# Down-projection in a fused two-block kernel: block sums by adding transfers, pairs of block buffers, one more turn by seven products

## The reference

```python
h2 = rmsnorm_2(x, norm2_g[l])
u = causal_dwconv(jnp.einsum('bsd,df->bsf', h2, w_up[l]), conv_w[l], conv_b[l])
u_gate, u_val = u[..., :D_FF], u[..., D_FF:]
x = x + jnp.einsum('bsf,fd->bsd', jax.nn.silu(u_gate) * u_val, w_down[l])
```

## Time and profile before

| | |
|---|---|
| median of 3 runs | 2071.07 us (2070.58 to 2071.88) |
| profiled execution | 2070.34 us, its span 2068.3 us |
| PE busy | 2062.9 us, 9896 matmuls |
| DVE busy | 1657.0 us |
| ACT busy | 1172.5 us |
| POOL busy | 51.8 us |
| HBM read | 420.57 MB, 204 GB/s over the span |

### The profile page before, as it was taken

How to read it: one execution, slowest core, us unless ns; L and a number is a source line. 1 busy time by engine, 2 the same in 40 slices (tenths; PEclk the granted TensorE clock), 3 DMA queues, 4 the chain that set the end, 5 groups by cost and what they waited for, 6 DMA issues and landing times.

```text
span 2068.3 us, 25511 instructions
## 1 busy us (share of the span) xinstructions
PE 2062.9 (100%) x9896; PEld 1732.2 (84%) x9896; DVE 1657.0 (80%) x1864; ACT 1172.5 (57%) x1398; POOL 51.8 (3%) x55
## 2 busy tenths in 40 slices
PE   9999999999999999999999999999999999999999
PEld 7888888888888887888888888888888888888887
DVE  7888788887887876887788778867777777789986
ACT  6766555555556555656555555555555555555553
POOL 0000000000000000110000000000000000000000
PEclk9999999999999999999999999999999999999999
DMA  9667777787674667655565656455555565556663
GB/s 348 206 199 225 222 233 226 210 244 221 247 263 153 218 207 213 207 179 182 154 231 180 210 182 218 160 184 181 188 190 191 190 195 183 192 184 233 226 202 131
DMA packets 118007, 424.33 MB, mean 205 GB/s; under 512 B 13184, under 2 KB 13952, under 8 KB 117632
## 3 DMA queue, kind: packets, MB, share of 16 engines
q1 hardware_dynamic: 109440, 394.66, 56.5%
q0 software_dynamic: 5472, 19.93, 5.6%
q10 hardware_dynamic: 2976, 8.14, 1.1%
HBM read 420.57 MB, written 2.10 MB: 204 GB/s over the span
## 4 chain that ended last, share of the span: by engine, by line
PE 99%; DMA 0%; ACT 0%; DVE 0%; ACTq 0%; issue 0%; DVEq 0%
PE g L938 51%; PE xs L984 10%; PE xs L791 8%; PE g L791 8%; PE g L988 7%; PE g L762 4%; PE xs L797 4%; PE g L797 4%; PE xs L840 1%; PE xs L1025 1%; PE xs L1161 0%; PE g L963 0%; PE xs L1158 0%; DMA par<-in_params 0%; PE xs L1178 0%; PE xs L1102 0%
## 5 line engine op out<-in xcount | busy, mean ns | idle before, releaser
L1859 DVE TENSOR_TENSOR w_lo<-raw,w_hi 128x1024 fp32r<-128x1024 f32 x625 | 757.3, 1221 | 290.9 <-ACT w_hi L1364 283.2
L1364 ACT ACTIVATE w_hi<-raw 128x1024 fp32r<-128x1024 f32 x625 | 655.7, 1057 | 508.4 <-PE g L938 221.6
L938 PE MATMUL g<-w_hi,in_both 128*128 128x512 f32 x1104 | 350.5, 390 | 0.0
L938 PE MATMUL g<-w_hi,mid_both 128*128 128x512 f32 x928 | 300.2, 393 | 0.0
L938 PEld LDWEIGHTS g<-w_hi,in_both 128*128 128x128 f32 x1104 | 207.3, 188 | 42.9
L938 PE MATMUL g<-w_lo,in_both 128*128 128x512 f32 x552 | 214.8, 389 | 0.0
L938 PEld LDWEIGHTS g<-w_hi,mid_both 128*128 128x128 f32 x928 | 174.2, 188 | 36.2
L938 PE MATMUL g<-w_lo,mid_both 128*128 128x512 f32 x464 | 180.6, 389 | 0.0
L791 PE MATMUL g<-mlp_both,w_hi 128*128 128x512 f32 x704 | 167.0, 391 | 0.0
L791 PE MATMUL xs<-mlp_both,w_hi 128*128 128x512 f32 x704 | 165.6, 390 | 0.0
L791 PEld LDWEIGHTS xs<-mlp_both,w_hi 128*128 128x128 f32 x704 | 130.7, 188 | 26.2
(11 more groups left out here) (532 smaller groups left out, 3439.5 us busy)
## 6 DMA issues: line engine op xcount, KB each, us to landing
raw<-in_stream SPq DMA_DIRECT2D x625, 512.0 KB, 4.3
d_block<-in_stream SPq DMA_DIRECT2D x28, 512.0 KB, 4.5
o_block<-in_stream SPq DMA_DIRECT2D x24, 512.0 KB, 4.7
v_block<-in_stream SPq DMA_DIRECT2D x20, 512.0 KB, 4.7
gm_block<-in_stream SPq DMA_DIRECT2D x16, 512.0 KB, 5.6
ge_block<-in_stream POOLq DMA_DIRECT2D x15, 512.0 KB, 5.5
ge_block<-in_stream SPq DMA_DIRECT2D x10, 512.0 KB, 4.6
gl_block<-in_stream POOLq DMA_DIRECT2D x6, 512.0 KB, 5.4
```

The source lines that it names most:

```text
L938: ins = mm(GG[:, bank, :], a[:, kt, t * P:(t + 1) * P], w[:, slot, half_chunk(j)], start=n == 0 and opens(item, bank), stop=ended and n == ...
L1364: activation(w_hi[:, n % RING, :], of[:], ACT.Copy).then_inc(hi_ready, 1)
L1859: v.tensor_tensor(w_lo[:, n % RING, :], of, w_hi[:, n % RING, :].bitcast(F32), ALU.subtract).then_inc(lo_ready, 1)
```

## The change

The down phase gets the other form. In each turn by products two block sums are now transfers that add, and the other two stay on DVE. There are two pairs of block buffers, used in turn, and the loads for a turn by products are issued one such turn earlier (two ahead in place of one). The four chunks of a mixed step now all stand between product 5 and product 7, in the order `MIXED_SPREAD`. In column group 1 a fifth turn goes by products: turn 10 with the chunks of turn 8, while turn 7's chunks go with the products of turn 6. With it comes one more set of sums of f. Column group 0 keeps its three mixed steps.

```diff
     "down": (((3, None), (4, None), (8, None), (9, None), (5, 0), (6, 1), (7, 2), (10, None)),
-             ((3, 0), (7, None), (4, 1), (5, 2), (8, 6), (9, None), (10, None))),
+             ((3, 0), (4, 1), (5, 2), (7, 6), (8, 10), (9, None))),
...
-SUMS_AT = {"v": (4, 8), "out1": (2, 6), "vv": (-7,), "down": (3, 7, 11, 64), "gm0": (-8, -5), "out2": (-7,)}
+SUMS_AT = {"v": (4, 8), "out1": (2, 6), "vv": (-7,), "down": (3, 7, 11, 64, 76), "gm0": (-8, -5), "out2": (-7,)}
...
-SPREAD = ("ug", "vv", "side")
+SPREAD = ("ug", "vv", "side", "down")
+TWO_SUMS = ("vv", "side", "down")
...
 MIXED = (1, "C0", 5, 7, "C1", 6, 3, "C2", 4, 2, "C3")
...
+MIXED_SPREAD = (1, 5, "C0", "C1", "C2", 3, "C3", 7, 6, 2, 4)
...
+def second_pair(q):
+
+    return QUADS[q][0] == "down" and (q - quads_ahead("down")) % 2 == 1
...
 def buffer_of(q, b):
 
+    if QUADS[q][0] == "down":
+        return b + 2 * second_pair(q)
...
-                if next_in_place(item) is not None and quad_of(item) + 1 < len(QUADS):
-                    q = quad_of(item)
-                    if QUADS[q + 1][0] == item.phase:
+                after = 2 if item.phase == "down" else 1
+                if next_in_place(item) is not None and quad_of(item) + after < len(QUADS):
+                    q = quad_of(item) + after
+                    if QUADS[q][0] == item.phase:
                         sp.wait_ge(lo_ready, n + 1)
-                        load_block(q + 1, next_in_place(item))
+                        load_block(q, next_in_place(item))
...
-                elif item.phase in MID_ORDER and item.product == 2:
+                elif item.phase in TWO_SUMS and item.product == 2:
                     dve.wait_ge(lo_ready, n + 1)
-                    to = wide(item.phase, item.group).blocks[B11]
+                    to = wide(item.phase, item.group).blocks[buffer_of(quad_of(item), B11)]
                     v.tensor_tensor(to[:], to[:], raw[:, CHUNK_COUNT[n] % RING, :], ALU.add).then_inc(sem["block_sums"], 1)
```

More of the change, by code:

```diff
@@ L282, in loads_of_block @@
 def loads_of_block(q, b):
-    return sum(phase not in SPREAD or b in (B11, B12) for phase, _, _ in QUADS[:q + 1])
+    return sum(not second_pair(k) and (QUADS[k][0] not in SPREAD or b in (B11, B12)) for k in range(q + 1))
+def second_pair(q):
+    return QUADS[q][0] == "down" and (q - quads_ahead("down")) % 2 == 1
 def spread_quads(q):
@@ L310, in sums_made @@
 def sums_made(q, p):
-    ahead = sum(1 if phase == "ug" else 2 if phase in MID_ORDER else 4 for phase, _, _ in QUADS[:q])
-    return ahead + ({5: 1, 4: 2} if QUADS[q][0] in MID_ORDER else {5: 1, 7: 2, 6: 3, 4: 4})[p]
+    ahead = sum(1 if phase == "ug" else 2 if phase in TWO_SUMS else 4 for phase, _, _ in QUADS[:q])
+    return ahead + ({5: 1, 4: 2} if QUADS[q][0] in TWO_SUMS else {5: 1, 7: 2, 6: 3, 4: 4})[p]
 def buffer_of(q, b):
+    if QUADS[q][0] == "down":
+        return b + 2 * second_pair(q)
     return b if b == B21 or QUADS[q][0] in SPREAD else (b + q - quads_ahead(QUADS[q][0])) % 3
@@ L652, in build, with block_in @@
     block_full = [sem[f"block_full{b}"] for b in range(4)]
+    second_full = [sem[f"second_full{b}"] for b in (B11, B12)]
+    def block_in(q, b):
+        if second_pair(q):
+            return second_full[b], 16 * ((q - quads_ahead("down")) // 2 + 1)
+        return block_full[b], 16 * loads_of_block(q, b)
     hi_ready, lo_ready, mm_done = sem["hi_ready"], sem["lo_ready"], sem["mm_done"]
@@ L699, in _ @@
                     sp.wait_ge(lo_ready, n + 1)
-                    if item.phase in MID_ORDER and item.product == 2:
+                    if item.phase in TWO_SUMS and item.product == 2:
                         sp.wait_ge(sem["block_sums"], sums_made(quad_of(item), 4))
@@ L730, in _ @@
                         sp.wait_ge(sem["y_ready"], GROUPS)
-                    load_block(QUADS.index((phase, of[0], MID_TURN)) if of else quads_ahead(phase), b)
+                    if of and phase == "down":
+                        load_block(quads_ahead(phase) + of[0], b)
+                    else:
+                        load_block(QUADS.index((phase, of[0], MID_TURN)) if of else quads_ahead(phase), b)
                 if n in GAIN_AT:
@@ L1351, in high_of_chunk @@
                     if item.product in (1, 3, 2):
-                        act.wait_ge(block_full[b], 16 * loads_of_block(q, b))
-                    elif item.phase in SPREAD and item.product != 5 and not (item.phase in MID_ORDER and item.product == 4):
+                        act.wait_ge(*block_in(q, b))
+                    elif item.phase in SPREAD and item.product != 5 and not (item.phase in TWO_SUMS and item.product == 4):
                         act.wait_ge(sem[f"block_added{item.product}"], 16 * spread_quads(q))
@@ L2597, in add_block @@
                     pool.wait_ge(lo_ready, n + 1)
-                p.dma_start(wide(item.phase, item.group).blocks[to][:], stream[block_row(q, b)], accum_op=ALU.add).then_inc(
+                p.dma_start(wide(item.phase, item.group).blocks[buffer_of(q, to)][:], stream[block_row(q, b)], accum_op=ALU.add).then_inc(
                     sem[f"block_added{product}"], 16)
```

19 lines of the change are left out of this document (10 added, 9 removed).

## The result

| | before | after |
|---|---|---|
| median of 6 runs | 2070.70 us (2070.36 to 2071.88) | 2086.04 us (2085.51 to 2088.76) |
| profiled execution | 2070.34 us, span 2068.3 | 2085.51 us, span 2083.7 |

The kernel became slower by 15.3 us: the ratio is 1.0077, with a 95% interval of 1.0067 to 1.0087. The forecast was 2079.1 us in 2076.5 to 2082.5, so the direction held and the size did not: +15.3 measured, +8.1 forecast. In the two longest runs of after, 2087.24 and 2088.76 us, the mean granted clock was 0.998; in the other four it was 1.00.

The account below looks back on a forecast made before the run. PE, at 99% of the chain, was taken to bound the kernel. Six seams of 1.57 us (9.42) less 1.36 us of PE work gave +8.06 on 2071.07, so 2079.1 us, range 2076.5 to 2082.5.

Parts of the forecast that it names:

- PE's work: Column group 1: the fifth turn by products makes 48 matmuls 42, 1.36 us less PE work.
- The seam: Between adjoining mixed steps, six products together: PE waits 1.57 us before product 5, at six places, 9.42 us.
- The rule on weight loads: At product 5: loads pulled ahead would make a seam some 0.11 us shorter, sum 7.4; the forecast followed the row instead.
- Product 7 and 6: Adding transfers for these items land at 7.9 us at most and stay hidden, 5.6 us of room for 7.
- The clock: Rival: after each of the six waits PE runs a stretch at 1.2 GHz, adding 16 us, 2095 us; chance 0.02.
- The upper end of a seam, 2.1 us: At each seam: a DVE slip of one operation adds 0.3 to 0.4 us, given 0.7 to 0.8 of room.
- the other parts: Adding transfers, traffic, block loads and sums of f beside the seams: all hidden, nothing added.
- the load of C3: Chunk load with least room on SP: issued at 12.1 us, lands at 16.6, wanted at 19.5; costs nothing.
- The check against traffic: Mixed step: ten transfers of 0.52 MB, 239 GB/s, held against 230 in the "ug" phase beside a full PE.
- the sums of f: Fifth set, 2.85 us of DVE, behind chunks or product 3: costs nothing, or 1 to 3 us once.
- the longer link: In the seam's way, low part to sum: 1.26 us taken, 1.36 the longer value; two such links add up to 0.2.
- transfers late: Rival: adding transfers land at 15.8 us, product 7 is 2.3 us late in 8 steps, 2097 us; chance 0.04.

Follow-up runs that it names:

- e10_spread_even: Changed kernel with step order 1, C0, 5, C1, C2, 7, 3, 6, 2, C3, 4 and sums of f at 67 and 78: 2085.29 us.
- e5_four_turns: Changed kernel without the fifth turn by products, with the steps of the kernel before in the new form and order: 2080.17 us, ratio 1.0047.
- e2_small_adds: Changed kernel with the down phase's adding transfers cut to 128 of 1024 columns, waits and order kept: 2080.52 us, ratio 1.0049.
- e13_copies_for_adds: Changed kernel with the down phase's adding transfers as plain copies of the same size from the same queue: 2080.69 us, ratio 1.0052.
- e7_fifth_turn_only: Kernel before with only the fifth turn by products added, its sums of f at items 64 and 76: 2071.59 us, ratio 1.0006.
- e3_sums_early: Changed kernel with the fourth and fifth sums of f at items 62 and 73 in place of 64 and 76: 2084.56 us, ratio 1.0069.

## Why the forecast was wrong in size

The right parts first.

- *PE's work.* 9890 matmuls, 1.36 us less: right.
- *The seam.* Six waits before product 5, at the six places named; each of its links as forecast but one, which took the longer of its two values. With the restart a bare seam costs 1.68 us where 1.57 was forecast: 0.6 us over six.
- *The rule on weight loads.* By it a seam would have been some 0.11 us shorter. The row decided against it, and rightly: at the first seam the weight load stands at 1901.81 and its matmul at 1901.82, 1.27 us after DVE's low part of 1.22 us began.
- *Product 7 and 6.* No wait before either: right, and `e10_spread_even` shows that the cover is real and needed.
- *The clock.* The rival was given 2%. It did not happen in the profiled execution of after, where the clock was 1.00 throughout the window. It did in single executions of other versions (`e5_four_turns`, some 1.6 us, and `e10_spread_even`), and the mean clock of 0.998 in two of after's six runs would fit it; their traces were not taken, so that stays open.

- *The upper end of a seam, 2.1 us.* It took 0.7 to 0.8 us of room for 4 and 1 from a slip of DVE, where the forecast's own lines give 0.46 and 0.68 (6.80 - 6.34 and 8.16 - 7.48). And such room is no help for product 5, since the whole way to it gets longer. In the fifth seam of `e2_small_adds` the low part of 2 started 2.01 us after its high part in place of 1.09, and this slip of 0.92 us cost 0.85 us of idle PE before 4 and 5 together.

**The step that failed** is the one on the other parts: the load of C3 "is issued behind the low part of C0, which ends at 9.71 + 1.14 + 1.22 = 12.1, lands at 16.6, and is wanted at 21.97 - 2.47 = 19.5. So nothing there." The term was put at nothing, and 4.6 us stood there. The issue time held (12.20 measured in the step behind the first seam). The rest failed in three respects at once.

1. *Landing.* It took 4.5 us from the earlier trace rows, where the loads had no adding transfer beside them. Here the two adding transfers of the step are issued just ahead of C3's load, and chunk loads took 6.5 us at the median and 8.4 at most. The check against traffic, 239 GB/s beside the 230 of the earlier trace rows, looked at the wrong quantity: bytes were fine (`e13_copies_for_adds`), engine time was not.
2. *Who wants it.* It held the landing against C3's own start on PE alone (19.5 is the last moment for that). ACT makes its high parts in order, so 7, 6, 2 and with 2 the whole way of the seam stand behind C3's. A load that lands in time for C3's matmuls, as at 19.10, can still be late for the seam.
3. *Room.* The items 4 and 1 had 0.46 and 0.68 us of room in the forecast. Any later start of that way uses these up, and then shows as a wait before 4 and as a seam of 1.98 us.

The next term failed too, at a smaller price: the sums of f, which "stand right after the low parts of chunks or product 3 [...]: nothing", or 1 to 3 us once. They have part of the waits in two steps (0.85 us even with small transfers, as above), and making them earlier gave 1.4 us back.

After's 16.4 us of idle PE against the forecast's terms:

| part | us | from |
|---|---|---|
| six seams as forecast | 9.4 | 6 x 1.57 |
| the longer link in each | 0.6 | 6 x 0.10 |
| late chunk loads, in part only together with the sums of f | 4.6 | after less `e2_small_adds` (4.5 less `e13_copies_for_adds`) |
| sums of f, start of group 1, rest | 1.8 | what `e2_small_adds` keeps beside its bare seams |
| sum | 16.4 | |

Less 1.36 us of PE work that is 15.0; the span grew by 15.4. The rest is the tail: 2083.7 - 2079.7 = 4.0 from the last matmul's start to the end, in place of 3.5. In after the first 512 KB store of the result leaves 0.95 us ahead of the last matmul's start, in place of 3.75. One plain turn fewer at the end is not enough for that, as `e7_fifth_turn_only` has one too and a tail of 3.5. Seams and late loads are shown by kernels of their own, but the parts of the table do not add up in every order. Of the 4.6 us, 2.2 stand in the two seams with sums of f in them, where after has 3.0 us more than two bare seams, `e2_small_adds` 0.85, and `e3_sums_early` nothing (but 2.0 before C1). The 1.8 us is a remainder: that the sums of f have part of it rests on where these waits stand and on `e3_sums_early`; 0.6 us stands at 1958.82, at the start of group 1, where DVE adds up results of group 0 ahead of the low part, and was not tried by itself.

The range failed because its ends held only the spread of the seam's links and one slip of DVE, and nothing for a load that lands late. The rival "transfers late" had the right neighbour and the wrong victim: it priced the adding transfer that comes late, not the load that an adding transfer makes late.

## What to carry to other kernels

Where operands that depend on sums stand close together in the order, follow the way from a place set free to the last of them and hold it against the PE work beside it; from a profile of before this came out within 0.1 us in 11. Then do the same for each load on the way. Take its landing longer than in a trace without the new transfers: here the longest before, 6.8 us, would have left C3's load 0.6 us of room, and 8.4 was measured. Hold it against the engine that reads it first and against all that stands behind it in that engine's order, not against its own matmul. Room of 0.46 us, as product 4 had it, was no room here: a late load or a sum of f took it.

## What the runs showed of the hardware

- A transfer that adds to SBUF held the 16 DMA engines for 3.0 us per 512 KB, a copy of the same bytes for 1.6; with two such in each 22 us step the median landing of plain loads rose from 4.3 to 6.5 us, and with copies to 4.9.
- TensorE's granted clock fell to 1.2 GHz for some eight matmuls after a wait of 1.99 us in `e5_four_turns` and after one of 2.49 us in `e10_spread_even`. It stayed at 2.4 GHz after six waits of 1.6 to 2.0 us in the profiled execution of after, and after one of 2.40 us in `e10_spread_even`.
- After each of the seams' waits for DVE's low part, at a clock of 2.4 GHz, the second matmul came 0.34 us behind the first in place of 0.2267.
